# Expert rows turned back from the queries' input, and two more query weights loaded ahead

## The chip, the core and the metric

One NeuronCore of a Trainium2 chip runs the kernel. Its engines work side by side, each through its own list of instructions in order: TensorE (PE in the profile; weight loads apart as PEld), VectorE (DVE), ScalarE (ACT), GpSimd (POOL, which here issues the gathers) and SyncE (SP, which issues the plain loads). They wait for one another by semaphores. Transfers run on 16 DMA engines that all queues share. The metric is the device time of one execution in microseconds; less is better.

## What is computed

Two blocks over 256 tokens of width 1024, all in float32. The second block has two layers, and the change lies in the expert part of each of them, for the 256 tokens of the main stream:

```
h2 = rmsnorm(x, norm2_g) * (1 + scale) + shift             # [256, 1024]
q  = (h2 @ w_pq).reshape(256, 8, 2, 128)                   # 8 heads, two half queries each
s  = einsum("lhpd,hpkd->lhpk", q, peer_keys)               # 128 keys per half
top 16 of each half, 256 sums, top 16 of these -> 16 experts of 16384 per head and token
act = gate * gelu(einsum("tkd,td->tk", peer_down[ee], h2)) # 128 experts per token
x  = x + m5 * einsum("tk,tkd->td", act, peer_up[ee])
```

So each layer reads 256 x 128 rows of 2048 floats (an expert's down row and up row lie side by side).

## The kernel before

A planner in Python (`Plan`) puts named steps in one list; each engine's program walks through that list and writes out its own part of every step, so the order of the list is the order within every queue. `peer_x` (L1410) plans the expert part of one layer.

**Ahead of the first gather.** The last products of the token mixer (`tile_out`) give X one block of 128 tokens after the other. For each block ACT takes the row statistics (`row_stats`), POOL the root, ACT scales the rows into `h2` (`row_scale`), TensorE turns them in eight 128x128 transposes (`col_turn`, two PSUM banks), and ACT and DVE apply gain and shift per channel on the way out (`col_turn_out`). The result `hT` (channels by tokens) is the input of the queries. Queries 1 to 7 are made for all 256 tokens: 32 matmuls (`peer_q`, helper line L1657), a copy on ACT, 8 score matmuls (`peer_scores`, L2118), two copies on ACT. Query 0 is made in halves of 128 tokens (`query_tile`). Their weights (`wpq`, 1 MB each) go through a ring of three pieces (`wx[:3]`): 0 is loaded ahead of the part, 1 and 2 as soon as the mixer's weights have been used, and 3 to 7 each when the query three before it has been made. DVE ranks the scores head by head (`ranks`; heads of block 0, then of block 1), which gives 16 expert indices per head.

**The expert rows.** The dot products need `h2` as token rows with gain and shift applied. `modulated_rows` loads the three rows gain, shift and scale broadcast over 128 partitions (SP, 512 KB each), and DVE forms the rows: one instruction for the gain (`mod_gain`, L2388), two per block (`mod_row`, L2394 and L2396). The three rows lie in `places[-2:]`, the last two of five 8 KB pieces behind the small buffers.

**The loop over 256 gathers** (`steps`: block tt, expert k). `fetch_ahead` issues a gather (`fetch`, POOL, L2967; 128 rows of 8 KB, 1.05 MB) for every free slot. `down` (DVE, L2627) forms the dot product with `h2`. After every four rows `gelu` runs (DVE, tanh on ACT, `gelu_end` on DVE, L2606), and `rows_up` adds the four up rows on TensorE: ACT makes a diagonal matrix of the activations (L2930), four matmuls per row (L2128) add into two banks, and this sets the row's slot free, after which POOL can gather into it. Slots go round in order: three of `places`, four spare ones (three in layer 1), two weight pieces, and, from step 4 on, when DVE has made the second block of `h2`, the two of `places[-2:]`. From step 40 on layer 0 gives the four spare ones back to another stage; at step 44, when all queries have been made, three more are added. The generator `ask` makes the queries: queries 1 and 2 are made before the loop; at steps 4, 8, 12, ... to 44 `next(asking)` goes on with the rest, behind the `rows_up` of that step.

Of the kernel before, what the change touches and what calls it, by code (L numbers as in the profile page):

```python
# [7 lines left out]
P = 128  # L8
# [25 lines left out]
def by2(ap):  # L34
    return ap.rearrange("p (a n) -> p a n", a=2)
# [99 lines left out]
class Plan:  # L135
# [47 lines left out]
    def tick(self, name, by=1):  # L183

        self.counts[name] = self.counts.get(name, 0) + by
        return (self.sem(name), self.counts[name])

    def put(self, kind, **args):
        self.items.append((kind, args))
# [1151 lines left out]
    def peer_c(self, banks, wr, sm, start, size, gslots, l, X):  # L1341
# [65 lines left out]
        put("peer_add", m5=m5.ap[:, 0:1024], loaded=m5_ok, acc=h2, X=X, done=end)  # L1407
        self.c_ok, self.b_free = end, [end]

    def peer_x(self, banks, sm, start, size, l, X, side, spare, last):  # L1410


        put, tick, t = self.put, self.tick, self.t
        wr = Ring(self.wx[:3])
        early = [self.load(wr, t["wpq"][l, 0], 2048)]
        put("prefetch", ws=early[0:1])
        ar = Arena(self.big, start, size)
        h2 = ar.get(2048, (2, 1024))
        act, gat, eix = ar.get(256, (2, 128)), ar.get(256, (2, 128)), ar.get(256, (2, 128)).bitcast(U32)
        iot, gl = ar.get(16), ar.get(32)  # L1420
        hT = ar.get(2048, (8, 256))
# [8 lines left out]
        hT_ok = []  # L1430
# [5 lines left out]
        places = [ar.get(2048) for _ in range((ar.size - ar.at) // 2048)]  # L1436
        gain, shift = self.gcols[:, 4 * l + 1, :], self.mcols[:, 2 * l, 24:32]

        def stats(tt, ready):
            r = self.rstd_of(sm, tt, 1.0 / 1024, EPS)  # L1440
            put("row_stats", src=X[:, tt, :], dump=h2[:, tt, :], r=r, ready=ready)
            return r

        def scaled(tt, r, ready):
            done = tick("rows_scaled")
            put("row_scale", src=X[:, tt, :], dst=h2[:, tt, :], by=sm[:, 8 + tt:9 + tt], r=r, done=done, ready=ready)
            us = [Use(banks.banks[i]) for i in range(2)]
            return dict(h=h2[:, tt, :], us=us, dst=hT[:, :, tt * P:(tt + 1) * P], done=done, gain=gain, shift=shift,
                        cols_ok=self.cols_ok)

        def turned(args):
# [13 lines left out]
        self.x_ok = end()  # L1465
        score_tile()
        early += [self.load(wr, t["wpq"][l, i], 2048) for i in (1, 2)]
        put("prefetch", ws=early[1:])
        rows = self.modulated_rows(l, 0, 3, "norm2", h2, [places[-2][:, 0:1024], places[-2][:, 1024:2048], places[-1][:, 0:1024]],
                                   [self.x_ok])  # L1470

        def ask():
            score_tile = query_tile(1, early[0], None)
            yield
            score_tile()
            yield
            for i in range(1, 8):
                query(i, early[i] if i < 3 else None)
                yield
                begun = score_begun(i)  # L1480
                if i > 2:
                    yield
                score_end(*begun)
                if i < 3:
                    yield

        asking = ask()
        route = ranks(asking)
        next(route)
        second = scaled(1, stats(1, self.x_ok), self.x_ok)  # L1490
        next(route)
        put("col_turn", **second)
        next(route)
# [3 lines left out]
            next(asking)  # L1497
        for _ in range(2):
            next(route)
        for _ in range(4):  # L1500
            next(asking)
        modulated = rows(hT_ok[0] + hT_ok[1])
        for _ in range(2):
            next(modulated)
        m5, m5_ok = both, tick("d_m5_x", 16)
        if last:
            fw, fw_ok, dump = last.get(1024), tick("d_final", 16), last.get(1024)
# [4 lines left out]
        def more(ap, freed=None):  # L1512
            s = Slot(ap, self.sem(f"pair{len(pairs)}"))
            s.count, s.freed = self.pair_counts.get(len(pairs), 0), freed
            pairs.append(s)
            free.append(s)
# [8 lines left out]
        def lend(w):  # L1525
            more(w.ap, w.freed)
            lent.append((w, pairs[-1]))

        lend(self.wx[3])
        lend(self.wx[4])  # L1530
        def rows_modulated():

            next(modulated)
            for ap in places[-2:]:
                more(ap, (self.sem("mod_rows"), self.counts["mod_rows"]))

        def asked_all():

            put("load_row", dst=m5, src=self.mods[l, 0, 5:6, :].to_broadcast([P, 1024]), done=m5_ok, before=[ended["keys"]])
            lend(self.wx[2])  # L1540
            more(hT.rearrange("p a b -> p (a b)"), ended["hT"])
            more(keys.rearrange("p a b -> p (a b)"), ended["keys"])
# [48 lines left out]
        for n, (tt, k) in enumerate(steps):  # L1591
            fetch_ahead()
            s, slot, _ = ahead.pop(0)
            if n == 4:
                rows_modulated()
            read = tick("rows_read")
            put("down", row=s.ap[:, 0:1024], full=s.full, h=h2[:, tt, :], out=act[:, tt, k:k + 1], done=read)
            batch.append((s, slot, k))
            if pending:
                rows_up(*pending.pop(0))  # L1600
            if 4 <= n < 48 and n % 4 == 0:
                next(asking, None)
            if n == 44:
                assert next(asking, None) is None
                asked_all()
            if (tt, k) in ends:
                while (tt, k // 16) not in gates_ok:
                    next(route)
                m = len(batch)
                at = 0 if at + m > 32 else at  # L1610
                mine = slice(k + 1 - m, k + 1)
                args = dict(at=act[:, tt, mine], u=gl[:, at:at + m], ag=ag[:, at:at + m], tanh=tick("gelu_tanh"))
                put("gelu", gat=gat[:, tt, mine], cubed=tick("gelu_cubed"), **args)
                at += m
                pending.append((tt, batch, args))
                batch = []
            if n < 6 or n % 5 in (1, 3):
                next(route, None)
            if n >= 64 and n % 12 == 4:
                assert not brief  # L1620
                next(side, None)
            if n == 128 + 12:
                add(0)
                if last:
                    r = final_stats(0)
            if last and n == 128 + 40:
                final_rows(0, r)
            if not last and n == 128 + 30:
                r = stats(0, self.x_ok)
            if not last and n == 128 + 60:  # L1630
                done = tick("rows_scaled")
                put("row_scale", src=X[:, 0, :], dst=h2[:, 0, :], by=sm[:, 8:9], r=r, done=done)
                first = self.first_turn(l + 1, h2[:, 0, :], done, [Use(banks.banks[i]) for i in (4, 5)], False)
            if not last and n == 252:
                put("col_turn", **first)
            yield 1.5
# [42 lines left out]
def tensor_program(pe, p):  # L1679
# [234 lines left out]
    def col_turn(h, us, done, r=None, **_):  # L1914
        for g, u in enumerate(us):
# [6 lines left out]
                pe.wait_ge(*done)  # L1922
            turn(u, [h[:, (4 * g + i) * P:(4 * g + i + 1) * P] for i in range(4)]).then_inc(u.full[0], 1)

    def low_begun(w, wt, hT, ready, n, u, **_):
        opened(u)
        for ok in ready:
            pe.wait_ge(*ok)
        pe.wait_ge(*w.full)
        tokens_first(pe, u, wt, hT, n=n, tiles=(0,))  # L1930
# [191 lines left out]
    def up_pe(row, full, d, diag, us, k, done, **_):  # L2122
# [8 lines left out]
        if k < 127:  # L2131
# [5 lines left out]
                 v_in=v_in, rope_in=rope_in, scores=scores, score_v=score_v, head_turn=group_turn,  # L2137
                 branch_gate=branch_gate, branch_out=branch_out, mix_out=mix_out, ffn_in=ffn_in, ffn_begun=ffn_begun, ffn_second=ffn_second,
                 ffn_out=ffn_out, ffn_last=ffn_last, mod=mod,
                 mod_columns=mod_columns, col_turn=col_turn, low_begun=low_begun, low_rank=low_rank, zp=zp, zp_ended=zp_ended,  # L2140
                 low_turn=low_turn, key_rope=key_rope, key_roped=key_roped,
                 kv_up=kv_up, kv_up_made=kv_up, q_made=q_made, q_roped=q_roped, att_score=att_score, att_turnp=att_turnp, att_out=att_out, att_turn=att_turn, fourier=fourier, pool=pool,
                 token_gate=token_gate, mix=mix, token_out=token_out, tile_begun=tile_begun, tile_out=tile_out, peer_q=peer_q,
# [8 lines left out]
def vector_program(v, p):  # L2152
# [469 lines left out]

    rows_read, act_done = [0], [0]

    def down(row, full, h, out, done):
        v.wait_ge(*full)
        v.tensor_tensor_reduce(row, row, h, 1.0, 0.0, ALU.mult, ALU.add, out).then_inc(done[0], 1)  # L2627
        rows_read[0] = done[1]
# [36 lines left out]
    def final(X, by, fw, r, loaded, normed, **_):  # L2665
# [9 lines left out]
                 mod_columns=mod_columns, row_scale_v=row_scale_v, col_turn_out=col_turn_out, low_rank_mid=low_rank_mid, low_turn_out=low_turn_out, key_roped=key_roped, kv_up=kv_up, kv_up_out=kv_up,  # L2675
# [11 lines left out]
def scalar_program(s, p):  # L2687
# [151 lines left out]
    def kv_up(K, ku, at, **_):  # L2839
        for j, u in enumerate(ku, at):  # L2840
            s.wait_ge(*u.full)
            s.copy(K[0:64, 2 * j:2 * j + 2, :], by2(u.ap[0:64, :])).then_inc(u.free[0], 1)

    def q_made(Q, u, **_):
        s.wait_ge(*u.full)
        s.copy(Q, by2(u.ap[0:96, :])).then_inc(u.free[0], 1)
# [79 lines left out]
    def up_pe(d, by, ready, diag, **_):  # L2926
        s.wait_ge(*ready)
        if d.before:
# [4 lines left out]
    kinds = dict(consts=consts, row_stats=row_stats, row_scale=row_scale, dt=dt, conv_in=conv_in, conv_end=conv_end, gate_in=gate_in,  # L2933
                 xs_turn=xs_turn, heads=heads, group_stats=group_stats, v_in=v_in, score_v=score_v, head_turn=head_turn,
                 branch_gate=branch_gate, ffn_in=ffn_in, mod_c=mod_c, context_in=context_in, col_turn_out=col_turn_out,
                 low_rank_out=low_rank_out, low_rank_scale=low_rank_scale, key_rope_out=key_rope_out, key_roped=key_roped, kv_up=kv_up, kv_up_out=kv_up, q_made=q_made,
                 att_out=att_out, att_turn=att_turn, att_turnp=att_turnp, att_score=att_score, fourier=fourier, zp=zp, zp_ended=zp,
                 token_gate=token_gate, peer_q_out=peer_q_out, peer_scores_out=peer_scores_out, peer_q_tile_out=peer_q_tile_out,
                 peer_scores_tile_out=peer_scores_tile_out, gates=gates, gelu=gelu,
# [279 lines left out]
```

## Time and profile before

| | us |
|---|---|
| median of 3 runs | 3985.13 (3985.05 to 3985.81) |
| profiled execution | 3982.54 |
| its span, first to last instruction | 3981.2 |
| busy on PE / DVE / ACT / POOL | 3595.6 / 2311.8 / 660.1 / 1290.0 |
| first gather of layer 0 / of layer 1 | 2343.56 / 3291.63 |

The page of the profile shows what each engine did over the whole span; a busy share is an average over stages with different limits, so the part that the change touches is read from tables of stretches and from the timelines of single engines. Times in these are microseconds from the first instruction.

### The profile page before, as it was taken

The numbers are of one execution on the slowest core, as the hardware profiler recorded it, in microseconds if no ns is written. First come the engines' busy times: TensorE is split into PE (matmuls) and PEld (weight loads), VectorE is DVE, ScalarE is ACT, GpSimd is POOL, SyncE is SP. The second block draws the span as 40 slices with busy tenths as digits, with TensorE's granted clock in tenths as the row PEclk, the third lists the DMA queues.
The fourth block names the chain that finished last, engine by engine and source line by source line (L and its number), as shares of the span: only waits on it lengthen the run. The fifth ranks groups of instructions, "written<-read, shape, count | busy, mean of one in ns | idle before, by whom it ended". The sixth has DMA issues, their size and how long they took to land. (4 is left out here: it accounts for less than half of the span.)

```text
span 3981.2 us, 41040 instructions
## 1 busy us (share of the span) xinstructions
PE 3595.6 (90%) x14568; PEld 2545.8 (64%) x14568; DVE 2311.8 (58%) x5462; ACT 660.1 (17%) x1804; POOL 1290.0 (32%) x1130
## 2 busy tenths in 40 slices
PE   8998999989999999999999979778879998877777
PEld 6667788878876888888847866333336785433333
DVE  3342013566877887775762157787763227777875
ACT  2232101110001330100002212111112211111111
POOL 1100000023445456774640013444441003444442
PEclk9999999999999999999999989889999999999999
DMA  8752344357998889998983369999996239999997
GB/s 329 290 204 84 128 151 188 127 206 291 345 355 344 293 305 408 405 410 343 413 327 121 111 237 384 416 413 411 413 420 254 106 130 373 404 420 419 420 419 327
DMA packets 207707, 1208.65 MB, mean 304 GB/s; under 512 B 23569, under 2 KB 24737, under 8 KB 95889
## 3 DMA queue, kind: packets, MB, share of 16 engines
q0 software_dynamic: 154976, 858.34, 53.8%
q1 hardware_dynamic: 52528, 347.69, 23.0%
q8 instruction: 118, 1.93, 0.2%
q14 instruction: 85, 0.69, 0.0%
HBM read 1204.79 MB, written 1.15 MB: 303 GB/s over the span
## 5 line engine op out<-in xcount | busy, mean ns | idle before, releaser
L1657 PE MATMUL bank<-big 128*128 128x256 f32 (+4 forms) x8888 | 1907.9, 374 | 40.9 <-issue 7.7
L1657 PEld LDWEIGHTS bank<-big 128*128 128x128 f32 (+2 forms) x8888 | 1627.6, 190 | 332.5 <-issue 82.1
L2967 POOL DMA_INDIRECT big<-in_pboth,big x1024 | 1218.2, 1190 | 1314.6 <-PE bank L2128 661.2
L2128 PE MATMUL bank<-big 128*128 128x512 f32 x2048 | 990.1, 641 | 246.0 <-ACT big L2930 245.9
L2627 DVE CUSTOM_DVE_ANT_0 big<-big 128x1024 f32<-128x1024 f32 x768 | 925.3, 1223 | 326.2 <-DMA big<-in_pboth,big 323.5
L2128 PEld LDWEIGHTS bank<-big 128*128 128x128 f32 x2048 | 410.0, 205 | 807.3 <-issue 484.2
L2638 DVE SCALAR_TENSOR_TENSOR big<-big 128x1024 f32<-128x1024 f32 x254 | 326.2, 1284 | 75.7 <-DMA big<-in_pboth,big 59.5
L2954 POOL TENSOR_TENSOR big<-big 128x1 f32<-128x1 f32 (+1 forms) x49 | 43.0, 877 | 912.0 <-DVE big L2186 911.8
L2930 ACT ACTIVATE big<-big 128x128 f32<-128x128 f32 x512 | 165.6, 391 | 276.3 <-DVE big L2606 266.9
L2920 ACT ACTIVATE big<-big 128x4 f32<-128x4 f32 (+2 forms) x134 | 27.6, 206 | 740.3 <-DVE big L2602 740.2
L1837 PE MATMUL bank<-big 128*128 128x256 f32 x576 | 129.5, 378 | 0.0
L1692 PE MATMUL bank<-big 128*128 128x128 f32 x596 | 92.6, 288 | 38.8 <-ACT big L2713 21.3
L1837 PEld LDWEIGHTS bank<-big 128*128 128x128 f32 x576 | 108.8, 189 | 15.8
L1866 PE MATMUL bank<-big 128*128 128x512 f32 x256 | 110.6, 592 | 1.7 <-DVE big L2353 1.7
L1844 PE MATMUL bank<-big 128*128 128x256 f32 x448 | 106.1, 390 | 6.0 <-DVE big L2302 4.6
L1692 PEld LDWEIGHTS bank<-big 128*128 128x128 f32 x596 | 74.6, 153 | 54.3 <-issue 35.9
L2474 DVE TENSOR_REDUCE big<-bank 128x1 f32<-128x512 f32 (+1 forms) x48 | 28.9, 602 | 138.4 <-PE bank L1998 138.3
L2339 DVE SCALAR_TENSOR_TENSOR big<-big,bank 128x256 f32<-128x256 f32 x32 | 13.5, 422 | 156.7 <-PE bank L1844 156.6
L2978 POOL DMA_DIRECT2D big<-in_iota x1 | 0.6, 584 | 308.7 <-DVE big L2510 308.7
L1844 PEld LDWEIGHTS bank<-big 128*128 128x128 f32 x448 | 86.9, 195 | 20.2 <-DVE big L2302 5.1
L2243 DVE SCALAR_TENSOR_TENSOR big<-bank,big 128x255 f32<-128x255 f32 (+1 forms) x144 | 62.7, 477 | 62.4 <-ACT big L2727 60.7
L2262 DVE SCALAR_TENSOR_TENSOR big<-big,bank 128x512 f32<-128x512 f32 x32 | 22.0, 688 | 127.0 <-ACT big L2742 126.7
(217 smaller groups left out, 2286.0 us busy)
## 6 DMA issues: line engine op xcount, KB each, us to landing
big<-in_w SPq DMA_DIRECT2D x104, 1024.0 KB, 7.8
big<-in_wmod POOLq DMA_DIRECT2D x48, 1024.0 KB, 8.1
big<-in_wgu SPq DMA_DIRECT2D x44, 1024.0 KB, 8.3
big<-in_wzg SPq DMA_DIRECT2D x36, 1024.0 KB, 4.8
big<-in_wro SPq DMA_DIRECT2D x32, 1024.0 KB, 7.1
big<-in_wpq SPq DMA_DIRECT2D x24, 1024.0 KB, 7.0
big<-in_wd SPq DMA_DIRECT2D x22, 1024.0 KB, 8.4
big<-in_pboth,big POOLq DMA_INDIRECT x1024, 11.1
```

Of the source, the lines that this page charges most:

```text
L1657: last = pe.matmul(o, a, b, start=(i == 0), stop=(i == n - 1))
L1692: last = pe.transpose(o[:, i, :], b, ident)
L1837: pe.matmul(u.ap[:, 0:256], wk[:, k, :], YT[:, k, :], start=(k == 0), stop=False)
L1844: last = pe.matmul(u.ap[:, 0:256], wk[:, k, :], YT[:, k, :], start=False, stop=(k == 15))
L1866: last = pe.matmul(u.ap, act[:, 2 * i + k, tt * P:tt * P + P], wk[:, k, 512 * n:512 * n + 512], start=(i + k == 0), stop=False)
L2128: last = pe.matmul(u.ap, d.ap, row[:, 512 * i:512 * i + 512], start=(k == 0), stop=(k == 127))
L2243: i = v.scalar_tensor_tensor(c[:, m, s:256], o[:, m, 0:256 - s], conv["w"][m][:, 3 - s:4 - s], c[:, m, s:256], ALU.mult, ALU.add)
L2627: v.tensor_tensor_reduce(row, row, h, 1.0, 0.0, ALU.mult, ALU.add, out).then_inc(done[0], 1)
L2638: v.scalar_tensor_tensor(at, s.ap, by, at, ALU.mult, ALU.add).then_inc(done[0], 1)
L2930: s.activation(d.ap, p.ident, ACT.Copy, scale=by).then_inc(diag[0], 1)
L2954: g.tensor_tensor(r.sm[:, 8 + r.at:8 + r.at + r.n], r.sm[:, 4 + r.at:4 + r.at + r.n], r.sm[:, 12:13].to_broadcast([P, r.n]), ALU.pow).then ...
L2967: g.indirect_dma_start(out=s.ap, out_offset=None, in_=table, in_offset=bass.IndirectOffsetOnAxis(ap=index, axis=0)).then_inc(s.full[0], 16)
```

## The change

The token rows `h2` are no longer formed by DVE from loaded rows. A new step `row_back` turns `hT` back: eight transposes on TensorE into two banks, two copies of 128x512 on ACT into `h2`. It is put once per block: for block 0 between `row_stats` and `row_scale` of block 1, for block 1 behind the queries that precede the loop. The first `down` of each block waits for its copies. `mod_load`, `mod_gain` and `mod_row` are gone from this part (they stay in the other stream's `peer_c`).

The two pieces set free take the weights of queries 3 and 4, whose loads are put ahead of those of 1 and 2. Four queries (1 to 4) instead of two are made ahead of the loop. Both pieces become row slots once queries 3 and 4 have been made; they stand at the same place in the order of slots as before. The rest of the queries is spread over steps 4, 10, 16, ... 40.

```diff
         early += [self.load(wr, t["wpq"][l, i], 2048) for i in (1, 2)]
-        put("prefetch", ws=early[1:])
-        rows = self.modulated_rows(l, 0, 3, "norm2", h2, [places[-2][:, 0:1024], places[-2][:, 1024:2048], places[-1][:, 0:1024]],
-                                   [self.x_ok])
+        if not self.wq:
+            self.wq = [Slot(ap, self.sem(f"wq{i}")) for i, ap in enumerate(places[-2:])]
+        for i, s in enumerate(self.wq, 3):
+            s.freed = self.mixed
+            early.append(self.load(Ring([s]), t["wpq"][l, i], 2048))
+        put("prefetch", ws=[*early[3:], *early[1:3]])
+
+        def rows_back(tt):
+            us = [Use(banks.banks[i]) for i in (2, 3)]
+            put("row_back", src=hT[:, :, tt * P:(tt + 1) * P], us=us, dst=h2[:, tt, :], ready=hT_ok[tt])
+            return [u.free for u in us]
...
             for i in range(1, 8):
-                query(i, early[i] if i < 3 else None)
+                query(i, early[i] if i < 5 else None)
                 yield
                 begun = score_begun(i)
-                if i > 2:
+                if i > 4:
                     yield
                 score_end(*begun)
-                if i < 3:
+                if i < 5:
                     yield
...
-        second = scaled(1, stats(1, self.x_ok), self.x_ok)
+        r1 = stats(1, self.x_ok)
+        rows_ok = [rows_back(0)]
+        second = scaled(1, r1, self.x_ok)
...
-        for _ in range(4):
+        for _ in range(8):
             next(asking)
-        modulated = rows(hT_ok[0] + hT_ok[1])
-        for _ in range(2):
-            next(modulated)
+        rows_ok.append(rows_back(1))
...
-        def rows_modulated():
-
-            next(modulated)
-            for ap in places[-2:]:
-                more(ap, (self.sem("mod_rows"), self.counts["mod_rows"]))
-
+        for s in self.wq:
+            more(s.ap, s.freed)
...
-            if n == 4:
-                rows_modulated()
             read = tick("rows_read")
-            put("down", row=s.ap[:, 0:1024], full=s.full, h=h2[:, tt, :], out=act[:, tt, k:k + 1], done=read)
+            put("down", row=s.ap[:, 0:1024], full=s.full, h=h2[:, tt, :], out=act[:, tt, k:k + 1], done=read,
+                rows_ok=rows_ok[tt] if k == 0 else ())
...
-            if 4 <= n < 48 and n % 4 == 0:
+            if 4 <= n < 44 and n % 6 == 4:
                 next(asking, None)
...
+    def row_back(src, us, ready, **_):
+        for ok in ready:
+            pe.wait_ge(*ok)
+        for g, u in enumerate(us):
+            opened(u)
+            turn(u, [src[:, 4 * g + i, :] for i in range(4)]).then_inc(u.full[0], 1)
...
+    def row_back(us, dst, **_):
+        for g, u in enumerate(us):
+            s.wait_ge(*u.full)
+            s.copy(dst[:, 512 * g:512 * g + 512], u.ap).then_inc(u.free[0], 1)
```

The first `row_back` is TensorE's, the second ACT's.

## Rows read from the trace of the kernel before

**Rows 1.** The page, part 2: moved bytes in 40 equal slices of the span

```profile
GB/s 329 290 204 84 128 151 188 127 206 291 345 355 344 293 305 408 405 410 343 413 327 121 111 237 384 416 413 411 413 420 254 106 130 373 404 420 419 420 419 327
```

**Rows 2.** Stretches: length, busy us (instructions) PE PEld DVE ACT POOL, PEclk, DMA share, GB/s

```profile
2344.00:2376.00 32.00, 19.97 (x102) 17.22 (x101) 22.85 (x60) 4.26 (x13) 10.78 (x10) 0.87 0.97 392
2376.00:2404.00 28.00, 28.00 (x83) 15.65 (x84) 23.40 (x72) 5.20 (x17) 11.98 (x10) 0.92 0.96 357
2376.00:2500.00 124.00, 117.00 (x376) 68.59 (x376) 86.08 (x254) 22.81 (x73) 50.56 (x44) 0.97 0.95 379
2500.00:2640.00 140.00, 111.52 (x240) 47.04 (x240) 109.57 (x323) 25.62 (x82) 63.89 (x57) 0.92 1.01 419
3292.00:3322.00 30.00, 18.55 (x100) 15.79 (x98) 21.94 (x58) 3.54 (x10) 8.87 (x9) 0.89 0.96 381
3322.00:3350.00 28.00, 27.35 (x82) 15.66 (x83) 22.69 (x71) 5.60 (x18) 12.31 (x11) 0.93 0.94 362
3322.00:3450.00 128.00, 124.09 (x392) 71.73 (x392) 91.90 (x269) 24.10 (x78) 58.61 (x52) 0.99 0.98 395
```

**Rows 3.** Timeline of POOL: start, duration, instruction [idle before <- what ended it]

```profile
2343.56 1.01 POOL L2967 DMA_INDIRECT big<-in_pboth,big  x1 [8.94 <-DVE big L2576]
...
2354.46 0.96 POOL L2967 DMA_INDIRECT big<-in_pboth,big  x1 [0.30 <-issue]
2374.18 1.80 POOL L2967 DMA_INDIRECT big<-in_pboth,big  x1 [18.76 <-DVE big L2396]
...
2379.79 0.94 POOL L2967 DMA_INDIRECT big<-in_pboth,big  x1 [2.51 <-PE bank L2128]
...
2488.12 0.94 POOL L2967 DMA_INDIRECT big<-in_pboth,big  x1 [15.25 <-PE bank L2128]
...
3321.08 1.81 POOL L2967 DMA_INDIRECT big<-in_pboth,big  x1 [18.82 <-DVE big L2396]
```

**Rows 4.** Timeline of SP's queue, layer 0

```profile
2298.51 0.43 SPq L3045 DMA_DIRECT2D big<-in_iota  x1
...
2332.48 0.91 SPq L3033 DMA_DIRECT2D big<-mods  x2
2346.93 67.07 SPq L3000 DMA_DIRECT2D big<-in_wpq  x5
```

**Rows 5.** Timeline of PE, layer 0; the last row is layer 1's query 2

```profile
2336.00 1.94 PE L1692 MATMUL bank<-big 128*128 128x128 f32 x8 [4.92 <-ACT big L2713]
2340.28 6.62 PE L1657 MATMUL bank<-big 128*128 128x128 f32 x32 [2.34 <-DVE big L2429]
...
2347.97 7.10 PE L1657 MATMUL bank<-big 128*128 128x256 f32 x32
...
2356.86 7.10 PE L1657 MATMUL bank<-big 128*128 128x256 f32 x32
2364.78 1.13 PE L2118 MATMUL bank<-big 128*128 128x128 f32 x8 [0.82 <-ACT big L2893]
2375.74 9.39 PE L2128 MATMUL bank<-big 128*128 128x512 f32 x16 [9.83 <-ACT big L2930]
...
2413.47 7.03 PE L2128 MATMUL bank<-big 128*128 128x512 f32 x16
...
3303.70 7.10 PE L1657 MATMUL bank<-big 128*128 128x256 f32 x32
```

**Rows 6.** Timeline of ACT, layer 0

```profile
2334.70 1.15 ACT L2713 ACTIVATE big<-big 128x1024 f32<-128x1024 f32 x1 [1.43 <-POOL big L2954]
...
2355.16 0.59 ACT L2893 COPY big<-bank 128x512 f32<-128x512 f32 x1 [6.50 <-PE bank L1657]
```

**Rows 7.** Timeline of DVE, layer 0

```profile
2372.68 1.23 DVE L2396 TENSOR_TENSOR big<-big 128x1024 f32<-128x1024 f32 x1
...
2375.09 0.16 DVE L2606 SCALAR_TENSOR_TENSOR big<-big 128x4 f32<-128x4 f32 x1
```

**Rows 8.** A stretch with the clock at its lower level, columns as in rows 2

```profile
2336.00:2340.00 4.00, 1.94 (x8) 1.54 (x8) 3.83 (x14) 1.51 (x4) 0.00 (x0) 0.50 0.53 218
```

More of the change, by code:

```diff
@@ L1408, in peer_c @@
         self.c_ok, self.b_free = end, [end]
+    wq = ()
     def peer_x(self, banks, sm, start, size, l, X, side, spare, last):
@@ L2139, in tensor_program @@
                  ffn_out=ffn_out, ffn_last=ffn_last, mod=mod,
-                 mod_columns=mod_columns, col_turn=col_turn, low_begun=low_begun, low_rank=low_rank, zp=zp, zp_ended=zp_ended,
+                 mod_columns=mod_columns, col_turn=col_turn, row_back=row_back, low_begun=low_begun, low_rank=low_rank, zp=zp, zp_ended=zp_ended,
                  low_turn=low_turn, key_rope=key_rope, key_roped=key_roped,
@@ L2623, in vector_program, with down @@
     rows_read, act_done = [0], [0]
-    def down(row, full, h, out, done):
+    def down(row, full, h, out, done, rows_ok=()):
+        for ok in rows_ok:
+            v.wait_ge(*ok)
         v.wait_ge(*full)
@@ L2935, in scalar_program @@
                  branch_gate=branch_gate, ffn_in=ffn_in, mod_c=mod_c, context_in=context_in, col_turn_out=col_turn_out,
-                 low_rank_out=low_rank_out, low_rank_scale=low_rank_scale, key_rope_out=key_rope_out, key_roped=key_roped, kv_up=kv_up, kv_up_out=kv_up, q_made=q_made,
+                 low_rank_out=low_rank_out, low_rank_scale=low_rank_scale, key_rope_out=key_rope_out, key_roped=key_roped, kv_up=kv_up, kv_up_out=kv_up, q_made=q_made, row_back=row_back,
                  att_out=att_out, att_turn=att_turn, att_turnp=att_turnp, att_score=att_score, fourier=fourier, zp=zp, zp_ended=zp,
```

## The prediction, made before the result was known

> **What bounds the kernel now.** I read the page first, then stretches, then single engines. The page's second part says that the ends of both layers run at 404 to 420 GB/s [rows 1]: these are the two expert phases, in which 256 gathers of 1.05 MB per layer (one row of the expert table for each of 128 tokens) are fetched. The table of stretches shows the plateau: 419 GB/s at a DMA share of 1.01 over 140 us [rows 2]. So one gather, or one query weight of the same size, costs 1.0486 MB / 419 GB/s = 2.50 us there, and the phase ends when its bytes are through: its length is bytes plus the time in which DMA starved. Before the plateau there is starvation: 379 GB/s from 2376 to 2500 us is 124 x (1 - 379/419) = 11.8 us lost in layer 0, 395 GB/s from 3322 to 3450 is 128 x (1 - 395/419) = 7.3 us lost in layer 1 [rows 2]. The timeline of POOL says why: nine gathers go out from 2343.56 to 2355.4, the tenth only at 2374.18, when DVE has made the second block of expert rows (L2396) and set its memory free, the twelfth at 2379.79, when TensorE has added up the first rows (L2128); and one waits 15.25 us until 2488.12 [rows 3]. That last wait is slot arithmetic: eleven row slots go round in order, so rows 36 to 39 lie in slots 3 to 6, the four spare ones that layer 0 gives back; the batch that ends them sets nothing free, and the next gather waits for row 40, while TensorE is late by five queries. Layer 1 has three spare pieces, thus eight gathers at first and the ninth at 3321.08 [rows 3].
>
> **The change, part by part.** Times are of the profiled execution.
>
> *Expert rows by transposes instead of by DVE.* Gone per layer: three 512 KB row loads, the last two issued at 2332.48 [rows 4], in a stretch ahead of the first gather, where DMA has room: worth nothing. Gone on DVE: one gain and four row instructions of 1.23 us [rows 7], 6.2 us per layer; but DVE then waits for head 1's scores, and, below, for a tanh, so nothing of it is late: I count zero. Added: twice eight transposes and two ACT copies. The eight transposes of `col_turn` took 1.94 us at clock 0.50 [rows 5, 8], so 1 us at full clock; a copy of 128x512 took 0.59 us [rows 6]. The first two copies stand before `row_scale`, which waited 1.43 us for POOL [rows 6]: 1.18 us fits, so the first gather stays at 2343.56. If the cover failed, at most 1.2 us per layer would show. No gain is possible there, since nothing was taken off that chain.
>
> *Weights 3 and 4 loaded early.* They join SP's queue right behind the iota load of 2298.51, which waits for the same token [rows 4], and ahead of weights 1 and 2, which went at that time anyway not before TensorE freed their slots. Of five loads from 2346.93 on [rows 4] three are left. Two pieces per layer leave the stretch in which DMA is full: 4 x 2.50 = 10.0 us less to move.
>
> *Five queries first, and the two slots.* This is the price. In before the order on TensorE is: queries 1 and 2, then batch 0 of the summed rows at 2375.74 [rows 5]. Now queries 3 and 4, and the second transposes, stand in between, and the tenth and eleventh gathers wait for those two queries instead of for DVE. A query starts every 8.89 us (2347.97, 2356.86) and takes 7.10 [rows 5]: query 3 runs 2365.75 to 2372.85, query 4 2374.64 to 2381.74, its scores end at 2383.7 (as query 2's at 2364.78 + 1.13 [rows 5], two periods on). Transposes 1 us: 2384.7. On ACT the score copies and the two row copies (0.59 us each [rows 6]) end at about 2385.5; behind them in ACT's queue stands the tanh of batch 0, and DVE, which reaches `gelu_end` at about 2372.6 (2375.09 less the two row instructions ahead of it [rows 7]), stands there until 2385.8, with every later `down` and rank behind it. `gelu_end` to the first matmul took 0.65 us (2375.09 [rows 7] to 2375.74): batch 0 starts at 2386.4. Four rows take 7.03 us [rows 5], about 1.72 each.
>
> So POOL's issues become 2372.9 (tenth), 2381.8 (eleventh), 2388.1 and on by 1.72 (twelfth to fifteenth). From issue to bytes I take 1.9 us, an estimate: 392 instead of 419 GB/s over 32 us [rows 2] is 2.1 us without bytes from 2344 on, 0.4 after the first issue, and part of it is ramp. DMA: 392 GB/s from 2344 to 2376 is 12.5 MB, that is nine gathers and three weights, so it is dry at 2376.1 [rows 2]; tenth gather to 2378.6; dry until 2383.7 (5.1 us); eleventh to 2386.2; dry until 2390.0 (3.8); four gathers to 2400.0. Then query 5 comes first (7.1 us), batch 1 is 2400.4 to 2407.3, its first slot free at 2402.1, bytes at 2404.0: dry 4.0. From there, going on in the same way (scores 5, batches 2 and 3, query 6, batch 4, ...), each release is 1 us or more ahead of need: 12.9 us lost in all. Batch 9 then ends at 2479.8, batch 10 releases row 40's slot at 2481.5, in time: the wait of 15.25 us is gone, since only three queries ran beside the batches. Layer 0: 12.9 instead of 11.8, +1.1. Layer 1 is the same 946.84 us later (query 2 at 3303.70 [rows 5]), with one gather less in hand: 381 GB/s from 3292 to 3322 is 11.4 MB of the eleven pieces [rows 2], dry at 3322.2; gaps 5.9, 3.8 and 4.1, 13.8 instead of 7.3, +6.5.
>
> The same walk over before gives 2.5 us for 2376 to 2404 and 2.75 for 3322 to 3350, where the rates (357 and 362 GB/s [rows 2]) say 4.1 and 3.8: a starved DMA loses somewhat more than the walk knows. I add the differences, 1.6 + 1.05 = 2.6 us.
>
> **Sum:** -10.0 + 1.1 + 6.5 + 2.6 = +0.2 us on a profiled execution of 3982.54 (span 3981.2); the median of the runs is 3985.13, so 3985.3, in round numbers 3985. Without the last term 3982.7.
>
> **The clock.** Query 0's second half ran 6.62 us from 2340.28 [rows 5]; the stretch before it had clock 0.50, the lower level (1.2 GHz), after TensorE had idled 4.92 us [rows 5, 8]. The first transposes now fill 1 us of that idle time. If they keep the clock up, that half takes 3.3 us, and everything that waits for queries 3 and 4 comes up to 3.3 us earlier per layer. Against it: in before eight transposes ran inside the slow stretch and did not lift it (1.94 us [rows 5]). The Trainium skill, "TensorE: Matmul & The Clock Gate", Part 4: PE-mode transpose, says that a transpose doesn't count as busy time for the clock; by that rule nothing is gained, by the plain reading 6.6 us; the rows here are too few to decide, and I take no gain.
>
> **The rivals.** *(A) No measurable change, about 3985*: the early gaps eat the 10 us. *(B) Faster, 3978.7*: the clock holds, 2 x 3.3 us come off. With the 2.6 us of the correction not there either, 3976. For it: the idle time shrinks by a fifth; against it: nearly 4 us of idle time stay. *(C) Slower, by DVE*: DVE stands some 13 us at the tanh, and is 10.7 us later at `gelu_end` than before (2385.8 against 2375.09). It was busy 23.40 of 28 us in 2376 to 2404 [rows 2], so it makes up 4.6 us in as many. TensorE is itself only 1.7 us later at batch 3 (2415.2 against 2413.47 [rows 5]). If batch 3's activations come after 2415.2, DVE is the bound. With 4.6 us made up it is 4.5 us late there, and the gather behind batch 4 starves 3.5 us per layer: 3992; with nothing made up, batches 3 and 4 cost 4 us each: 16 us, 4001. Middle: 3996. Against it: in that stretch of before DVE's idle time was partly waiting for gathers, which after a stall have long landed. *(D) The early loads do not help*, because they collide with query 0's weight and the keys: four pieces are 10 us from 2297, and TensorE asks for the first at about 2320, so it can't be; under 2 in 100.
>
> **How the numbers follow.** 0.2% (8 us) is about what a measurement can tell from no change. A has 0.62, B 0.18, C 0.20; D is in A. The likeliest one's own range is 3979 to 3991. For 8 in 10 I go down to B without the correction, 3976, and up to C's middle, 3996. Faster by over 0.2% (under 3977.2) needs B and more, or gaps shorter than I reckon: 0.17; slower by over 0.2% (over 3993.1): 0.19; the rest 0.64.
>
> **What the profile of the changed kernel would show.** Right if: POOL waits for a query's matmul (L1657's line) ahead of the tenth and eleventh gathers, near 2373 and 2382, and the twelfth leaves near 2388; DMA has holes near 2379 to 2384, 2386 to 2390 and 2400 to 2404, and none at 2482 to 2487; three query weights instead of five go out after 2346.93; DVE idles some 13 us on ACT's tanh. Wrong if: the first gather moves from 2343.56 (the copies were not covered); the clock in 2336 to 2346 is full (B); batch 3 waits for ACT's diagonals, and so for DVE (C); or if the holes are filled in a way that I did not see, as by a twelfth gather that doesn't wait for batch 0.

## The result, and the profile after

The changed kernel took 3990.68 us (median of 20 runs), the kernel before 3983.95 us (20 runs on the same chip): a ratio of 1.0019, interval 1.0013 to 1.0025 (here and below, ratios are not quotients of the medians; those differ from them by up to 0.07%). It is slower by 6.7 us; no change was forecast. The profiled execution of after took 3990.15 us (span 3988.9), 7.6 more than that of before (3982.54). On its time axis layer 0's first gather lies 1.5 us earlier than in before (2342.06), layer 1's 1.6 us later (3293.24); a stretch compared with [rows 2] is shifted by that much.

Stretches of after, columns as in [rows 2]:

```profile
2344.00:2376.00 32.00, 28.98 (x148) 24.86 (x147) 15.89 (x52) 4.57 (x12) 8.65 (x9) 0.99 1.00 411
2376.00:2404.00 28.00, 25.60 (x97) 16.80 (x96) 18.88 (x62) 6.92 (x22) 7.34 (x7) 1.00 0.59 217
2376.00:2500.00 124.00, 111.11 (x332) 60.68 (x330) 85.48 (x251) 22.33 (x73) 45.81 (x41) 0.94 0.86 344
2500.00:2640.00 140.00, 109.96 (x226) 45.73 (x227) 107.76 (x316) 25.79 (x82) 62.64 (x59) 0.90 1.01 419
3322.00:3350.00 28.00, 25.35 (x108) 18.49 (x109) 14.59 (x49) 6.64 (x21) 6.03 (x6) 1.00 0.66 252
3322.00:3450.00 128.00, 114.21 (x348) 63.94 (x349) 88.03 (x258) 24.08 (x80) 49.34 (x44) 0.95 0.89 358
```

The plateau is the same 419 GB/s, so a piece still costs 2.50 us there. Ahead of it DMA starves more: 217 GB/s from 2376 to 2404 us where [rows 2] has 357, and 252 where it has 362. TensorE idles longer too: 12.9 of 124 us instead of 7.0, though it has less to do there, as query 3 now lies ahead of the stretch.

Below, a hole is a stretch in which DMA runs dry, and a batch is the four rows that one `rows_up` adds (batch 0 is rows 0 to 3, batch 10 rows 40 to 43).

Timeline of POOL in after, as [rows 3]:

```profile
2342.06 1.01 POOL L2987 DMA_INDIRECT big<-in_pboth,big  x1 [8.94 <-DVE big L2589]
...
2352.90 0.94 POOL L2987 DMA_INDIRECT big<-in_pboth,big  x1 [0.30 <-issue]
2371.60 0.94 POOL L2987 DMA_INDIRECT big<-in_pboth,big  x1 [17.76 <-PE bank L1663]
2380.49 0.94 POOL L2987 DMA_INDIRECT big<-in_pboth,big  x1 [7.95 <-PE bank L1663]
2386.88 1.55 POOL L2987 DMA_INDIRECT big<-in_pboth,big  x1 [5.45 <-PE bank L2141]
...
2400.69 0.94 POOL L2987 DMA_INDIRECT big<-in_pboth,big  x1 [7.71 <-PE bank L2141]
...
2492.77 0.94 POOL L2987 DMA_INDIRECT big<-in_pboth,big  x1 [19.38 <-PE bank L2141]
```

Nine gathers go out at once; the tenth and eleventh wait for queries 3 and 4 (L1663), the twelfth for batch 0 of the summed rows (L2141). The last row is the wait that was forecast to vanish: it is 19.38 us long, where [rows 3] has 15.25.

Timeline of PE in after, then one row of DVE's:

```profile
2364.23 7.10 PE L1663 MATMUL bank<-big 128*128 128x256 f32 x32
2372.15 1.13 PE L2131 MATMUL bank<-big 128*128 128x128 f32 x8 [0.82 <-ACT big L2913]
2373.12 7.10 PE L1663 MATMUL bank<-big 128*128 128x256 f32 x32
2381.04 1.13 PE L2131 MATMUL bank<-big 128*128 128x128 f32 x8 [0.82 <-ACT big L2913]
2382.01 1.04 PE L1698 MATMUL bank<-big 128*128 128x128 f32 x8
2384.62 7.14 PE L2141 MATMUL bank<-big 128*128 128x512 f32 x16 [1.58 <-ACT big L2950]
2391.60 7.10 PE L1663 MATMUL bank<-big 128*128 128x256 f32 x32
2398.54 7.03 PE L2141 MATMUL bank<-big 128*128 128x512 f32 x16
...
2406.30 13.92 PE L2141 MATMUL bank<-big 128*128 128x512 f32 x32
...
2473.15 8.83 PE L2141 MATMUL bank<-big 128*128 128x512 f32 x16 [1.90 <-ACT big L2950]
2488.72 10.17 PE L2141 MATMUL bank<-big 128*128 128x512 f32 x16 [6.74 <-ACT big L2950]
```

```profile
2383.97 0.17 DVE L2619 SCALAR_TENSOR_TENSOR big<-big 128x4 f32<-128x4 f32 x1 [12.88 <-ACT big L2940]
```

Batch 0 starts at 2384.62 instead of 2375.74 [rows 5]: 8.9 us later (10.4 counted from the first gather), behind two queries, with TensorE busy from 2364.23 on but for 3.2 us (0.82 twice and 1.58). Batches 2 and 3 run through from 2406.30 (32 matmuls). Near 2488 TensorE stands idle for 6.74 us ahead of batch 10.

**The books.** In a stretch, (1 - rate / 419) x length is the time that DMA lost. By [rows 2] and the rows above, layer 0 lost 11.8 us before and 124 x (1 - 344/419) = 22.2 after; layer 1 lost 7.3 before and 128 x (1 - 358/419) = 18.6 after. That is 21.7 us more, less 10.0 for four pieces that no longer move there: +11.7. From first to last gather the phases grew by 3.5 us (670.53 to 674.03) and 8.6 (654.04 to 662.67), +12.1 together. Outside them 4.5 us came off (1.5 ahead of the first gather, 0.4 between the layers, 2.5 behind the last gather), in these two executions; the 1.5 are there already at SP's first load of the part (2295.09 against 2296.60), so nothing that the change does in layer 0's expert part gave them. Sum +7.6, up to rounding.

### The profile page after: what moved, and what is told of

Read it like the earlier page. It is cut to its first block and busy times, and to the rows that moved or that the text cites. A ratio compares the mean times of both kernels' runs of the same rounds, so it can differ in the third digit from the quotient of the medians.

```text
span 3988.9 us, 41092 instructions
## 1 busy us (share of the span) xinstructions
PE 3593.1 (90%) x14600; PEld 2543.7 (64%) x14600; DVE 2299.6 (58%) x5452; ACT 662.8 (17%) x1812; POOL 1288.0 (32%) x1130
## 5 line engine op out<-in xcount | busy, mean ns | idle before, releaser
L1663 PE MATMUL bank<-big 128*128 128x256 f32 (+4 forms) x8888 | 1907.5, 374 | 41.8 <-issue 7.7
L1663 PEld LDWEIGHTS bank<-big 128*128 128x128 f32 (+2 forms) x8888 | 1626.8, 190 | 330.1 <-issue 80.3
L2141 PE MATMUL bank<-big 128*128 128x512 f32 x2048 | 986.3, 639 | 253.1 <-ACT big L2950 253.1
L2141 PEld LDWEIGHTS bank<-big 128*128 128x128 f32 x2048 | 407.8, 204 | 818.3 <-issue 481.8
L2352 DVE SCALAR_TENSOR_TENSOR big<-big,bank 128x256 f32<-128x256 f32 x32 | 13.5, 422 | 155.7 <-PE bank L1850 155.7
```

The lines of the kernel that those rows point to most:

```text
L1663: last = pe.matmul(o, a, b, start=(i == 0), stop=(i == n - 1))
L2141: last = pe.matmul(u.ap, d.ap, row[:, 512 * i:512 * i + 512], start=(k == 0), stop=(k == 127))
```

## The experiments

The theories of the expectations: **Q, later T** (two more queries ahead of batch 0 starve DMA), **R** (transposes and copies themselves cost), **S** (what costs is that fewer slots are there at the start), and **L** (bytes of other loads lengthen the hand-back wait). Time that DMA lost, in us, worked out as above; the stretches are counted from each kernel's own first gather, so that frames don't matter. The ratios of the experiments are to 35 runs of before on the same chip as the experiment's own 11 or 12; the two chips give before 3982.70 and 3980.81 us. The lost times are of one execution each; like phases of like kernels (layer 1 of before and of the late hand-back on before, which only changes layer 0) differ by 2.0 us in length.

| kernel | 34 to 64, L0 | 34 to 64, L1 | 128 to 160, L0 | ratio to before (95%) |
|---|---|---|---|---|
| before | 2.9 | 1.6 | 6.4 | 1 |
| after | 13.5 | 13.4 | 8.9 | 1.0019 (1.0013 to 1.0025) |
| rows back only | 1.3 | 2.6 | 7.1 | 0.9987 (0.9977 to 0.9996) |
| queries 3, 4 in the loop | 5.1 | 4.4 | 6.3 | 0.9996 (0.9987 to 1.0005) |
| four queries first, nothing early | 8.4 | 8.9 | 9.0 | 1.0022 (1.0014 to 1.0031) |
| after, hand-back later | 12.4 | 13.3 | -0.1 | 1.0012 (1.0003 to 1.0021) |
| before, hand-back later | 3.0 | 3.2 | 2.1 | 0.9995 (0.9987 to 1.0004) |
| after, other loads later | 12.1 | 13.3 | 8.9 | 1.0022 (1.0013 to 1.0031) |
| rows back, hand-back later | 0.5 | 2.5 | 2.1 | 0.9980 (0.9971 to 0.9989) |
| in the loop, hand-back later | 4.9 | 4.0 | 2.9 | 0.9979 (0.9970 to 0.9988) |

**Rows back only.** Queries 3 and on go back into the loop, no weight is early, and the two pieces are slots from the start:

```diff
...
-        put("prefetch", ws=[*early[3:], *early[1:3]])
+        put("prefetch", ws=early[1:])
...
-                if i > 4:
+                if i > 2:
...
-        for _ in range(8):
+        for _ in range(4):
             next(asking)
...
-        for s in self.wq:
-            more(s.ap, s.freed)
+        for ap in places[-2:]:
+            more(ap, self.mixed)
...
-            if 4 <= n < 44 and n % 6 == 4:
+            if 4 <= n < 48 and n % 4 == 0:
```

> The expert rows come from the transposes, as in the change, but only queries 1 and 2 are made ahead of the loop, weights 3 to 7 go through the ring as before, and the two freed pieces are row slots from the start. Theory Q (the queries put ahead of the first batch cost the time): no query stands ahead of batch 0, and two more gathers go out at once, so DMA has 14 pieces (13 in layer 1) in hand instead of 12 (11) and 5 us more until it is dry; 2 to 4 us per layer come off the kernel before: 0.998 to 0.999 of it. Theory R (the transposes and copies themselves cost the time, on ACT or TensorE ahead of the first gather or in the loop): slower than before, 1.001 to 1.002, as the changed kernel.

Measured 3976.68 us against 3982.70 before. R falls: with all transposes and copies in, the kernel is faster than before. PE and POOL of this kernel:

```profile
2371.72 9.01 PE L2136 MATMUL bank<-big 128*128 128x512 f32 x16 [6.37 <-ACT big L2945]
```

```profile
2375.77 0.93 POOL L2982 DMA_INDIRECT big<-in_pboth,big  x1 [19.44 <-PE bank L2136]
```

The first wait of POOL is now the twelfth gather's, for batch 0, which begins at 2371.72: 4.0 us before that of [rows 5], and 2.5 us counted from the first gathers, which is what the two row instructions of DVE that stood ahead of it took (1.23 us each [rows 7]). The gain of some 5 us (0.13%, interval 0.04 to 0.23%) is more than DMA's losses account for: over the first 640 us of the phases they are 0.8 and 1.0 us shorter than in before. So Q's ratio came out, but not by Q's reckoning: the early holes of before, 2.9 and 1.6 us, were too small to give 2 to 4 us per layer, and in layer 1 that hole is longer now. Where the rest of the gain comes from is not settled.

**Queries 3 and 4 in the loop.** After, with their weights still early, but made at steps 4 and 12 like the others; the pieces become slots then.

> The changed kernel with one thing undone: queries 3 and 4 are made in the loop (steps 4 and 12) as in the kernel before, and their pieces join the row slots only then; their weights are still loaded ahead of the first gather. Theory Q: batch 0 starts near 2373 instead of 2385 in the trace's time, the early holes of DMA shrink from 13 to 5 to 8 us per layer, the 10 us of bytes stay saved: 0.998 to 0.9995 of the kernel before. Theory R: no better than the changed kernel, 1.001 to 1.002. Theory S (one or two row slots fewer at the start are what costs): worse than the changed kernel, over 1.002, since nine and eight slots are all that is there until query 3.

Measured 3978.86, ratio 0.9996: against R and S, which expected 1.001 and more, and just above Q's band. Q's early holes came out as expected (5.1 and 4.4 us), but not its "10 us of bytes stay saved". Against rows back only it moves two pieces (5.0 us) less per layer, yet the phases are as long: 665.52 and 653.44 us against 665.92 and 652.95. The losses of the first 160 us are 5.0 and 5.5 us longer (16.6 and 14.8 against 11.6 and 9.3). As much was lost in holes as the saved bytes would have taken. Here the early weights also keep two slots from the gathers until queries 3 and 4 have been made, and this pair of kernels can't tell the two apart; the next experiment can.

**Four queries first, nothing early.** The order of after, but weights 3 and 4 through the ring and both pieces slots from the start, so no gather waits for a query:

```diff
...
-        put("prefetch", ws=[*early[3:], *early[1:3]])
+        put("prefetch", ws=early[1:])
...
-                query(i, early[i] if i < 5 else None)
+                query(i, early[i] if i < 3 else None)
...
-        for s in self.wq:
-            more(s.ap, s.freed)
+        for ap in places[-2:]:
+            more(ap, self.mixed)
```

> The changed kernel's order (queries 1 to 4 ahead of batch 0 of the summed rows, query 5 behind it), but weights 3 and 4 come through the ring during the phase and the two pieces are row slots from the start, as in the rows-back-only kernel. So no gather waits for queries 3 and 4; only TensorE's order is that of the changed kernel. Theory T (TensorE's order alone starves DMA: every slot from the twelfth on waits for batch 0, at about 2385 instead of 2372): eleven gathers and four weights are 37.5 us of bytes from 2344, dry near 2381 until 2390, so 8 to 12 us are lost 34 to 64 us behind the first gather in each layer, against 1 to 3 in the rows-back-only kernel; DVE still stands some 12 us at the tanh; time about 3992, ratio 1.002 (1.001 to 1.0035). Theory S (the two slots that wait for queries 3 and 4 are what starves DMA): with these slots there from the start 2 to 5 us are lost there, and the time is near 3979, ratio 0.9985 to 1.0.

Measured 3989.09 against 3980.81: T, in time and in holes (8.4 and 8.9 us). Its POOL and its stretches:

```profile
2387.47 1.55 POOL L2982 DMA_INDIRECT big<-in_pboth,big  x1 [30.63 <-PE bank L2136]
```

```profile
2380.00:2384.00 4.00, 2.81 (x20) 2.17 (x18) 0.00 (x0) 1.79 (x5) 0.00 (x0) 1.00 1.00 401
2384.00:2388.00 4.00, 2.79 (x7) 1.35 (x8) 3.08 (x9) 1.91 (x7) 0.53 (x1) 1.00 0.28 117
2388.00:2392.00 4.00, 4.00 (x11) 1.79 (x10) 3.73 (x16) 0.21 (x1) 2.93 (x3) 1.00 0.59 172
```

The twelfth gather leaves at 2387.47, as after's (2386.88): POOL waits for batch 0 alone, and 30.63 us. DMA runs at its full rate until 2384, since the two weights that after has early are still to come; in after it moved 217 GB/s from 2376 to 2404. In both kernels eleven gathers go ahead of the twelfth, and it leaves 44.9 and 44.8 us behind the first, so after's two late slots cost nothing here. So of the 13.5 us in after, 8.4 are there by the order alone (7.1 more than in rows back only), and 5.1 are the early weights' own bytes (2 x 2.50 us), missing where nothing else could take their place. It also shows that S, as put for this run, falls.

**The hand-back later.** The four spare slots of layer 0 are handed back from step 48 on, in after and in before:

```diff
-                if slot in brief and n >= 40:
+                if slot in brief and n >= 48:
```

> The changed kernel, but layer 0 gives its four spare slots back from step 48 on instead of step 40. If the wait of 19.4 us for row 40 (a hole of some 9 us in DMA near 2484 to 2498) comes from all four slots going back in one batch while rows 40 to 43 are late, it goes, and the kernel is 6 to 9 us faster than the changed one: 0.9995 to 1.0005 of the kernel before. If the rows are late for another reason (DVE behind with ranks), the wait only moves and it stays at 1.0015 to 1.002.

> The kernel before with the same late handback (step 48 instead of 40). Its wait of 15.25 us for row 40 should go too: 4 to 7 us faster than before, 0.998 to 0.999. If it does, the handback is a cost that both kernels share and no part of the change.

Measured 1.0012 and 0.9995. The hole at 128 to 160 us closes in after (8.9 to -0.1) and shrinks in before (6.4 to 2.1), while the early holes of after stay (12.4, 13.3). By the ratios it is worth 0.07% in after and 0.05% in before (0.12 and 0.11 by the medians), each within its interval; expected were 6 to 9 and 4 to 7 us, that is 0.15 to 0.23 and 0.10 to 0.18%. With the later hand-back in both, after is still 0.17% slower than before; so the hand-back is a part of the loss and not the cause of the difference. From step 44 on three more slots are in the round (those of the third weight, the input's transposes and the keys); that this is why step 48 costs less is argued, not tried.

**Other loads later.** After, but SP sends the gain row and, queued behind it, two weights of the side work (1.70 MB in all: 512, 640 and 512 KB) not when the keys are read, but from step 60 on:

```diff
-            put("load_row", dst=m5, src=self.mods[l, 0, 5:6, :].to_broadcast([P, 1024]), done=m5_ok, before=[ended["keys"]])
...
+            if n == 60:
+                put("load_row", dst=m5, src=self.mods[l, 0, 5:6, :].to_broadcast([P, 1024]), done=m5_ok, before=[summed[0]])
```

> The changed kernel, but the gain row and what SP holds behind it (the next weights of the side work, 1.65 MB together) go out only when the rows of step 50 or so are summed, not when the keys are read. Theory L (the longer hand-back wait of 19.38 us comes from these bytes, which stand ahead of the gathers of rows 40 to 43): the hole 128 to 160 us behind the first gather falls from 8.9 us to about 5, the wait to about 15, the time by 3 us, ratio 1.001. Theory T (it comes from TensorE still being late by its queries): hole and wait stay within 1.5 us of 8.9 and 19.4, ratio 1.002.

Measured 3991.03, 1.0022. In after they stand ahead of the last gathers before the wait; here SP sends them at 2541.33. In before they went at 2486.15: the change, whose queries end sooner, had moved them up by some 20 us. Neither theory holds whole. First SP in before (one row) and in after, then the stretches around the hole, in after and in this kernel, and this kernel's hand-back wait, its batch 10, and two rows of its DVE:

```profile
2486.15 0.33 SPq L3041 DMA_DIRECT2D big<-mods  x1
...
2464.40 0.33 SPq L3061 DMA_DIRECT2D big<-mods  x1
2464.77 0.43 SPq L3020 DMA_DIRECT2D big<-in_wkv  x1
2465.24 0.43 SPq L3020 DMA_DIRECT2D big<-in_wukv  x1
```

```profile
2484.00:2488.00 4.00, 0.00 (x0) 0.00 (x0) 3.76 (x8) 0.00 (x0) 0.00 (x0) 0.58 0.79 326
2488.00:2492.00 4.00, 3.28 (x4) 1.52 (x5) 2.60 (x8) 1.50 (x5) 0.00 (x0) 0.50 0.03 10
2492.00:2496.00 4.00, 4.00 (x7) 1.58 (x6) 0.00 (x0) 0.00 (x0) 0.94 (x1) 0.64 0.40 98
```

```profile
2480.00:2484.00 4.00, 0.67 (x1) 0.50 (x2) 3.83 (x11) 1.12 (x4) 0.00 (x0) 0.75 0.54 225
2484.00:2488.00 4.00, 4.00 (x6) 1.59 (x5) 1.22 (x3) 0.38 (x2) 0.61 (x1) 0.50 0.00 0
2488.00:2492.00 4.00, 4.00 (x9) 1.72 (x9) 0.00 (x0) 0.00 (x0) 1.50 (x3) 0.90 0.75 246
```

```profile
2487.39 0.94 POOL L2990 DMA_INDIRECT big<-in_pboth,big  x1 [15.27 <-PE bank L2144]
```

```profile
2483.33 9.84 PE L2144 MATMUL bank<-big 128*128 128x512 f32 x16 [5.58 <-ACT big L2953]
```

```profile
2471.33 1.23 DVE L2645 CUSTOM_DVE_ANT_0 big<-big 128x1024 f32<-128x1024 f32 x1 [1.19 <-DMA big<-in_pboth,big]
...
2482.69 0.16 DVE L2622 SCALAR_TENSOR_TENSOR big<-big 128x4 f32<-128x4 f32 x1
```

The wait falls to 15.27 as L says, but the hole stays at 8.9 us: without the 1.70 MB DMA runs dry 4 us sooner, and refills as much sooner. T falls too: TensorE was not late, it idled 5.58 us ahead of batch 10. What it waited for is ACT's diagonals, and so DVE: the row at 2471.33 is DVE's last wait for a gather (row 41), and from there to batch 10's `gelu_end` at 2482.69 it works on without a wait, 6.2 us of it on ranks. The hole is the time from the last bytes in hand through DVE's list, ACT and batch 10 to the next gather; other bytes only push it.

**The best of both.** Rows back only, and queries in the loop with early weights, each with the hand-back at step 48:

> Rows back only (no early weights, two queries first, the two pieces slots from the start), and the four spare slots are handed back from step 48 on instead of 40. Expected: the 7.1 us hole 128 to 160 us behind the first gather falls to about 2, as it fell from 6.4 to 2.1 in the kernel before; the time by 3 to 4 us against rows back only: 3974, ratio 0.998 (0.997 to 0.999). If what stood behind that wait comes out later in the phase instead, it stays at 0.9987.

> Queries 3 and 4 in the loop with their weights loaded early, and the hand-back from step 48 on. Against the rows-back-only kernel with the same hand-back it moves two pieces per layer less (5.0 us at 419 GB/s) and has two slots less until queries 3 and 4 are made. If the bytes and the holes cancel (holes of 34 to 64 us were 5.3 and 5.7 us longer in layer 0 and 1 in all), the two kernels agree within 0.05%: ratio 0.9985. If early weights are worth their bytes once nothing else holds the gathers, it is 0.997; if the slots are worth more than the bytes, 0.9995 or above.

Measured 3973.63 and 3972.08 against 3980.81: both beat the kernel before by 0.2%, and by the two ratios after by some 0.4%. They don't differ beyond the intervals: early weights, with the two slots that they keep, are worth nothing here either. With them the losses of the first 160 us are 5.2 us longer in layer 0 and 6.5 in layer 1, for 5.0 us of bytes.

## Why the prediction was wrong, point by point

*Right: the places of the early waits.* The tenth, eleventh and twelfth gathers were forecast at 2372.9, 2381.8 and 2388.1; less the 1.5 us by which after's first gather lies earlier that is 2371.4, 2380.3 and 2386.6, and they came at 2371.60, 2380.49 and 2386.88. Batch 0, forecast 2386.4 (2384.9), began at 2384.62; DVE stood 12.88 us at the tanh. Three holes of 12.9 us, or 14.5 with the correction, were forecast for layer 0; from 2376 to 2404 us 28 x (1 - 217/419) = 13.5 were lost. The first gather did not move for the copies: it lies 1.50 us earlier than in before, as the second block's `col_turn` on TensorE does (2334.49 against 2336.00 [rows 5]). And -10.0 us for four pieces agrees with the books, where it closes them to 0.4 us.

*Wrong, first step: "the wait of 15.25 us is gone".* The walk had batch 10 release row 40's slot at 2481.5 because TensorE had fewer queries to do beside the batches. TensorE did have the time: it idled 6.74 us there. But batch 10 waited for its activations. First DVE and TensorE in before, then DVE in after:

```profile
2482.18 0.16 DVE L2606 SCALAR_TENSOR_TENSOR big<-big 128x4 f32<-128x4 f32 x1
...
2485.96 7.05 PE L2128 MATMUL bank<-big 128*128 128x512 f32 x16
```

```profile
2475.40 1.23 DVE L2642 CUSTOM_DVE_ANT_0 big<-big 128x1024 f32<-128x1024 f32 x1 [2.73 <-DMA big<-in_pboth,big]
...
2481.84 1.23 DVE L2642 CUSTOM_DVE_ANT_0 big<-big 128x1024 f32<-128x1024 f32 x1 [1.23 <-DMA big<-in_pboth,big]
...
2483.45 0.17 DVE L2615 SCALAR_TENSOR_TENSOR big<-big 128x4 f32<-128x4 f32 x1
...
2488.07 0.16 DVE L2619 SCALAR_TENSOR_TENSOR big<-big 128x4 f32<-128x4 f32 x1
```

In before DVE had batch 10's `gelu_end` done at 2482.18, and TensorE, behind query 7 and batch 9, began the batch only at 2485.96: TensorE was late, as the prediction says. In after the rows 41 and 43 of the batch came late (waits of 2.73 and 1.23 us), and between its `gelu` (last row 2483.45) and its `gelu_end` (2488.07) DVE's list holds a stretch of ranks and the `down` of row 44. Counted from the first gather, `gelu_end` came at 138.6 us in before and 146.0 in after, and batch 10 at 142.4 and 146.7. With the other loads later `gelu_end` came at 141.1 and the batch at 141.7: about 5 us of the delay are those loads, and the rest is there without them. The walk went on after 2404 with each release "1 us or more ahead of need"; from 64 to 128 us behind layer 0's first gather that held (DMA lost 0.2 us or less), but for batch 10 it counted TensorE alone, and not the rows' data and DVE. So the hand-back hole is 8.9 us where I reckoned none; before it was 6.4, and those 6.4 us were in the 11.8 that I took off as replaced.

*Wrong, second step: what the new holes replace.* In both layers I set the whole loss of before (11.8 and 7.3 us) against the new early holes alone (14.5 and 14.85 with the correction). Only what was lost early in before goes; the rest stays beside them. Layer 0: 4.1 early and 7.7 later before, 13.5 and 8.7 after. Layer 1: 3.8 and 3.5 before, 28 x (1 - 252/419) = 11.2 and 7.4 after (in part the end of the early holes, by the table 13.4 in 30 us; counted from the first gathers, 64 to 160 us lost 3.6 before and 4.4 after). Losses forecast: 29.35 us; measured 22.2 + 18.6 = 40.8. The 11.4 us between them are the miss in the phases; 4.5 us that came off outside them hid part of it in the total. That 3990.68 us lies inside the forecast's 3976 to 3996 says nothing for the sum, since one miss covers a part of the other.

*The rivals.* The clock (B) was not held. PE in after, and a stretch as in [rows 8]:

```profile
2329.41 1.16 PE L1698 MATMUL bank<-big 128*128 128x128 f32 x8
2334.49 1.94 PE L1698 MATMUL bank<-big 128*128 128x128 f32 x8 [3.93 <-ACT big L2728]
2338.77 6.62 PE L1663 MATMUL bank<-big 128*128 128x128 f32 x32 [2.34 <-DVE big L2442]
```

```profile
2336.00:2340.00 4.00, 1.66 (x9) 1.29 (x8) 3.83 (x14) 1.18 (x4) 0.00 (x0) 0.50 0.01 4
```

The first row's transposes fill 1 us of the gap, 3.93 us of idle time are left behind them, and the query's half takes the same 6.62 us as in [rows 5]. The Trainium skill, "TensorE: Matmul & The Clock Gate", Part 4: PE-mode transpose, says that a transpose in that mode doesn't count as busy for the clock in the same way; the 0.50 agrees, though it would also fit the idle time alone.

DVE's backlog (C): in layer 0 batches 2 and 3 ran without a break from 2406.30, so batch 3 waited for no activation; in layer 1 it waited 0.95 us for ACT's diagonals, far less than C's price of 3.5 us per layer. The time came out near C's band, but DVE's stand at the tanh is not why: what DVE holds up is batch 10, 100 us later. (D) is out by its reason: the early weights were there in time, as query 3 ran at 2364.23 straight behind query 2's scores. That the early loads do not help came true all the same, since their bytes came back as holes.

## What to carry to other kernels

In this kernel's phases, which are bound by bytes, bytes taken out of a stretch in which DMA is about to run dry were worth nothing: they came back as a hole of the same length, since nothing was at hand to fill it. Put first the work that sets buffers free; two queries of 8.9 us each moved ahead of it cost 7.1 us of DMA time in layer 0 and 6.3 in layer 1 (8.4 and 8.9 against 1.3 and 2.6), with all eleven (ten) row slots there from the start. When one engine is taken off a wait, look for the next one on it: at batch 10 DVE stood where TensorE had been. And when a forecast replaces one set of holes with another, split the old loss by place first, and take off only the part whose cause the change removes.

## What the runs showed that was not expected

The clock makes the hand-back hole longer. TensorE idled 5.58 us for DVE and ACT ahead of batch 10 in the kernel with the loads later, the granted clock from 2484 to 2488 us was 0.50, its lower level (1.2 GHz), and the batch took 9.84 us, where batch 1 of after took 7.03. From the batch's start to the gather that its first row lets go it took 4.06 us (2483.33 to 2487.39), and 4.05 in after; in before, where TensorE had no idle time ahead of batch 10 and the clock was 1.00, it took 2.16 (2485.96 to 2488.12 [rows 3]). So some 1.9 us of the hole are the clock's, an estimate from these rows. Batch 0 of rows back only took 9.01 us after 6.37 us of idle time, that of after 7.14 after 1.58.
